# Entry normalisation of a one-core encoder trunk: ScalarE measures four of nine tiles, VectorE centres and gains in one pass, ScalarE scales after it, GpSimd shifts last, and most mask constants are built later

## The reference, cut to what matters

```
def layer_norm(x, g, b):
    xf = x.astype(F32)
    mu = jnp.mean(xf, -1, keepdims=True)
    var = jnp.mean(jnp.square(xf - mu), -1, keepdims=True)
    return ((xf - mu) * lax.rsqrt(var + LN_EPS) * g.astype(F32) + b.astype(F32)).astype(x.dtype)

xp = layer_norm(x_prompt, ln_in_g, ln_in_b)      # (1, 1024, 1024)
xs = layer_norm(x_sample, ln_in_g, ln_in_b)      # (1, 64, 1024)
```

## Time and profile before

| what | value |
|---|---|
| median of three runs | 2655.39 us |
| span of the profiled execution | 2650.3 us (of the whole execution only this span is recorded) |
| TensorE busy with matmuls | 2431.2 us, 92% |
| VectorE, ScalarE, GpSimd busy | 1923.1, 1373.6, 1339.5 us |
| the entry: first transposition, end of the entry | 15.60 us, 63.64 us after the span's start |

### The profile page before, as it was taken

The page is one execution under the profiler, slowest core; times in us unless marked ns, Lnnn a source line. Parts: engine busy times, 40 slices in busy tenths (PEclk is TensorE's granted clock), DMA queues, the critical chain, the costliest instruction groups (busy, mean ns, idle before and its releaser), DMA issues. The chain is left out here.

```text
span 2650.3 us, 40161 instructions
## 1 busy us (share of the span) xinstructions
PE 2431.2 (92%) x14824; PEld 2183.7 (82%) x14824; DVE 1923.1 (73%) x3073; ACT 1373.6 (52%) x2032; POOL 1339.5 (51%) x1317
## 2 busy tenths in 40 slices
PE   4999999999999999999986999699999999999990
PEld 4889898898998989989875775499989898888980
DVE  7475765757758567575676687578888888888875
ACT  3443625426245263452633332267777777777772
POOL 6354664646546556455564265334555455554320
PEclk9999999999999999999987999799999999999995
DMA  5201111111110111101113323489999999999994
GB/s 183 61 26 33 54 34 45 34 40 46 42 45 28 39 45 39 57 25 41 45 73 115 102 75 134 119 261 285 311 305 310 302 303 311 307 313 313 352 333 162
DMA packets 207582, 380.77 MB, mean 144 GB/s; under 512 B 22694, under 2 KB 129546, under 8 KB 206874
## 3 DMA queue, kind: packets, MB, share of 16 engines
q1 hardware_dynamic: 180330, 302.31, 33.0%
q0 software_dynamic: 25824, 71.42, 11.8%
q10 hardware_dynamic: 1232, 4.46, 0.4%
HBM read 314.84 MB, written 72.97 MB: 146 GB/s over the span
## 5 line engine op out<-in xcount | busy, mean ns | idle before, releaser
L122 PE MATMUL ps<-xTh,w_mix_low 128*128 128x368 f32 (+1 forms) x1728 | 595.8, 345 | 10.2 <-POOL w_mix_low L116 8.8
L123 PE MATMUL ps<-xTl,w_mix_high 128*128 128x368 f32 (+1 forms) x1728 | 569.6, 330 | 0.0
L124 PE MATMUL ps<-xTh,w_mix_high 128*128 128x368 f32 (+1 forms) x1728 | 567.5, 328 | 0.0
L2087 POOL DMA_INDIRECT ys_d<-yo,tab_early x114 | 214.2, 1879 | 426.9 <-DVE yo L2259 263.9
L122 PEld LDWEIGHTS ps<-xTh,w_mix_low 128*128 128x128 f32 x1728 | 326.0, 189 | 21.9 <-issue 18.6
L123 PEld LDWEIGHTS ps<-xTl,w_mix_high 128*128 128x128 f32 x1728 | 326.2, 189 | 9.1 <-issue 6.2
L124 PEld LDWEIGHTS ps<-xTh,w_mix_high 128*128 128x128 f32 x1728 | 325.6, 188 | 0.0
L2129 PE MATMUL ps<-xghl,wgh 128*128 128x320 f32 (+5 forms) x1024 | 271.4, 347 | 13.5 <-DVE xghl L116 6.9
L2129 PE MATMUL ps<-xghl,wuh 128*128 128x320 f32 (+5 forms) x1024 | 263.4, 344 | 0.0
L2131 PE MATMUL ps<-xghl,wgl 128*128 128x160 f32 (+5 forms) x1024 | 240.0, 234 | 0.0
L2131 PE MATMUL ps<-xghl,wul 128*128 128x160 f32 (+5 forms) x1024 | 238.6, 233 | 0.0
(11 more groups left out here) (378 smaller groups left out, 5968.8 us busy)
## 6 DMA issues: line engine op xcount, KB each, us to landing
wd_early<-in_w_exp_down SPq DMA_DIRECT2D x64, 1024.0 KB, 9.2
wg_early<-in_w_exp_gate SPq DMA_DIRECT2D x124, 512.0 KB, 7.5
wu_early<-in_w_exp_up SPq DMA_DIRECT2D x124, 512.0 KB, 5.8
w_mix_raw<-in_w_in SPq DMA_DIRECT2D x72, 512.0 KB, 3.9
mT_d<-gs_m SPq DMA_DIRECT2D x8, 544.0 KB, 2.7
xr_m<-in_x_prompt SPq DMA_DIRECT2D x8, 512.0 KB, 3.7
xn_d<-xr_m SPq DMA_DIRECT2D x8, 512.0 KB, 2.8
out<-vrow_m SPq DMA_DIRECT2D x8, 512.0 KB, 4.8
```

The costliest lines, as they stand in the source:

```text
L122: pe.matmul(out, ll, rh, start=start, stop=False)
L123: pe.matmul(out, lh, rl, start=False, stop=False)
L124: return pe.matmul(out, lh, rh, start=False, stop=stop)
L2087: pool.indirect_dma_start(out=ys_d[:, :], out_offset=rows_of(e, j, m), in_=yo[:m, b, j, :], in_offset=None, compute_op=ALU.add, bounds_che ...
```

## The change

It does five things.

1. Tiles 1, 3, 5 and 7 are measured by ScalarE: a Copy over the tile with an accumulated sum (`entry_total`), a Copy of one column that makes the mean, a Square with the mean as bias and an accumulated sum (`entry_spread`). The even tiles keep bn_stats on VectorE, two tiles ahead of their use. Epsilon comes in as the bias of the square root.
2. VectorE subtracts the mean and multiplies by `g_in` in one scalar_tensor_tensor (`centre`); then it takes the reciprocal. The multiplication L1157 and the one-column instruction L1149 go.
3. ScalarE multiplies by the reciprocal after that (`entry_scale`), ahead of high(t-2) in its list, where the normalisation stood behind it.
4. GpSimd's shift waits for ScalarE's scaling. The first group of weights is split after shift(0), the second after shift(2), and the mask levels come behind shifts 5 to 8 and after the loop.
5. The statistics have a buffer of their own for each tile (`ste`).

```diff
+            BY_SCALAR = (1, 3, 5, 7)
...
+                def entry_total(t):
+                    m = rows(t)
+                    act.wait_ge(x_in[t % 4], 16 * (t // 4 + 1))
+                    act.activation(entry_dump[:m, :], xr[:m, t % 4, :], ACT.Copy, accum_out=ste[:m, t, 14:15]).then_inc(entry_sum, 1)
+
+                def entry_spread(t):
+                    m, n = rows(t), BY_SCALAR.index(t) + 1
+                    stt = ste[:m, t, :]
+                    act.wait_ge(entry_sum, n)
+                    act.activation(stt[:, 12:13], stt[:, 14:15], ACT.Copy, scale=1.0 / D).then_inc(entry_mean, 1)
+                    act.wait_ge(entry_mean, n)
+                    act.activation(entry_dump[:m, :], xr[:m, t % 4, :], ACT.Square, scale=-1.0, bias=stt[:, 12:13],
+                                   accum_out=stt[:, 13:14]).then_inc(entry_square, 1)
...
+                def entry_scale(t):
+                    m = rows(t)
+                    act.wait_ge(scaled, t + 1)
+                    act.wait_ge(inverse_ready, t + 1)
+                    act.activation(xr[:m, t % 4, :], xr[:m, t % 4, :], ACT.Copy, scale=ste[:m, t, 16:17]).then_inc(normed, 1)
+
+                act.wait_ge(memo, 4)
+                entry_total(1)
+                entry_root(0)
+                entry_spread(1)
                 for t in range(NT):
-                    m = rows(t)
-                    stt = st[:m, t % 2, :]
-                    act.wait_ge(var_ready, t + 1)
-                    act.activation(stt[:, 15:16], stt[:, 14:15], ACT.Sqrt).then_inc(rstd_ready, 1)
+                    if t + 1 < NT:
+                        if t and t + 1 in BY_SCALAR:
+                            entry_total(t + 1)
+                            entry_spread(t + 1)
+                        entry_root(t + 1)
+                    entry_scale(t)
                     if t >= 2:
                         high(t - 2)
-                    act.wait_ge(shift_ready, t + 1)
-                    act.activation(xr[:m, t % 4, :], xr[:m, t % 4, :], ACT.Identity, scale=stt[:, 16:17], bias=stt[:, 17:18]).then_inc(normed, 1)
...
+                def centre(t):
...
+                    dve.scalar_tensor_tensor(out=xr[:m, t % 4, :], in0=xr[:m, t % 4, :], scalar=stt[:, 12:13], in1=g_in[:m, :],
+                                             op0=ALU.subtract, op1=ALU.mult).then_inc(scaled, 1)
+                    dve.wait_ge(rstd_ready, t + 1)
+                    dve.reciprocal(stt[:, 16:17], stt[:, 15:16]).then_inc(inverse_ready, 1)
...
+                statistics(0)
                 for t in range(NT):
-                    statistics(t)
-                    if t >= 1:
-                        gain(t - 1)
-                    scale(t)
+                    centre(t)
+                    if t + 2 in by_vector:
+                        statistics(t + 2)
                     if t >= 2:
                         low(t - 2)
...
-                    pool.wait_ge(scaled, t + 1)
+                    pool.wait_ge(normed, t + 1)
...
                 for t in range(NT):
                     shift(t)
-                    if t == 0:
-                        split_due(0)
-                    if 1 <= t < 8:
-                        level(t - 1)
+                    if t in (0, 2):
+                        split_first()
+                    if t >= 5:
+                        level(t - 5)
+                for i in range(4, NL):
+                    level(i)
```

More of the change, by code:

```diff
@@ L354, in mixer @@
             tri = entry_only.enter_context(nc.sbuf_tensor("tri", [P, 2, P], F32))
+            ste = entry_only.enter_context(nc.sbuf_tensor("ste", [P, NT, 20], F32))
         x, pm = sb("x_m", [P, 2, NL + 1, 256]), sb("pm_m", [P, 2, NL + 1, P])
@@ L362, in mixer @@
                        "osb_copied pa pd diff_done exp_done eb_done qe_exp qe_done x_done p_done masked a_done ke_done ke_copied "
-                       "y_done oT_copied su_done s_done sg_done silu_done g_done squares root_ready u_raw merged wo_in wo_high wo_low last_s par_in xr0 xr1 xr2 xr3 var_ready rstd_ready entry_s shift_ready normed scaled xn_ready turned x_high x_low xs0 xs1 xs2 xs3 "
+                       "y_done oT_copied su_done s_done sg_done silu_done g_done squares root_ready u_raw merged wo_in wo_high wo_low last_s par_in xr0 xr1 xr2 xr3 var_ready rstd_ready entry_s inverse_ready entry_sum entry_mean entry_square scaled normed xn_ready turned x_high x_low xs0 xs1 xs2 xs3 "
                        "memo built lb_in lb_act lb_dve high_ready") as (block, (
@@ L368, in mixer @@
                 y_done, oT_copied, su_done, s_done, sg_done, silu_done, g_done, squares, root_ready, u_raw, merged, wo_in, wo_high, wo_low, last_s,
-                par_in, xr0, xr1, xr2, xr3, var_ready, rstd_ready, entry_s, shift_ready, normed, scaled, xn_ready, turned, x_high, x_low,
+                par_in, xr0, xr1, xr2, xr3, var_ready, rstd_ready, entry_s, inverse_ready, entry_sum, entry_mean, entry_square, scaled, normed, xn_ready, turned, x_high, x_low,
                 xs0, xs1, xs2, xs3, memo, built, lb_in, lb_act, lb_dve, high_ready)):
@@ L386, in mixer @@
             EARLY = 4
+            BY_SCALAR = (1, 3, 5, 7)
+            by_vector = [t for t in range(NT) if t not in BY_SCALAR]
+            entry_dump = oT[:, 0:D]
             def destination(kind, h, i):
@@ new lines, in entry_root @@
+                def entry_root(t):
+                    stt = ste[:rows(t), t, :]
+                    if t in BY_SCALAR:
+                        act.wait_ge(entry_square, BY_SCALAR.index(t) + 1)
+                        act.activation(stt[:, 15:16], stt[:, 13:14], ACT.Sqrt, scale=1.0 / D, bias=stt[:, 18:19]).then_inc(rstd_ready, 1)
+                    else:
+                        act.wait_ge(var_ready, by_vector.index(t) + 1)
+                        act.activation(stt[:, 15:16], stt[:, 13:14], ACT.Sqrt, bias=stt[:, 18:19]).then_inc(rstd_ready, 1)
@@ L1135, in statistics @@
                     m = rows(t)
-                    xt, stt = xr[:m, t % 4, :], st[:m, t % 2, :]
+                    xt, stt = xr[:m, t % 4, :], ste[:m, t, :]
                     dve.wait_ge(x_in[t % 4], 16 * (t // 4 + 1))
-                    if t >= 2:
-                        dve.wait_ge(normed, t - 1)
                     for b in range(2):
                         ch(dve.bn_stats(stt[:, 6 * b:6 * b + 6], xt[:, 512 * b:512 * b + 512]))
[L1142 to L1152, removed]
+                    dve.bn_aggr(stt[:, 12:14], stt[:, 0:12]).then_inc(var_ready, 1)
+                def centre(t):
                     m = rows(t)
+                    stt = ste[:m, t, :]
                     if t == 0:
                         dve.wait_ge(par_in, 32)
-                    dve.wait_ge(normed, t + 1)
-                    dve.tensor_tensor(xr[:m, t % 4, :], xr[:m, t % 4, :], g_in[:m, :], ALU.mult).then_inc(scaled, 1)
+                    if t in BY_SCALAR:
+                        dve.wait_ge(entry_square, BY_SCALAR.index(t) + 1)
+                    else:
+                        dve.wait_ge(var_ready, by_vector.index(t) + 1)
+                    dve.scalar_tensor_tensor(out=xr[:m, t % 4, :], in0=xr[:m, t % 4, :], scalar=stt[:, 12:13], in1=g_in[:m, :],
+                                             op0=ALU.subtract, op1=ALU.mult).then_inc(scaled, 1)
+                    dve.wait_ge(rstd_ready, t + 1)
+                    dve.reciprocal(stt[:, 16:17], stt[:, 15:16]).then_inc(inverse_ready, 1)
                 def low(t):
@@ L1165, in _ @@
                 ch = Chain(dve, entry_s)
+                dve.memset(ste[:, :, 18:19], LN_EPS).then_inc(memo, 1)
                 dve.memset(tri[:, :, :], 1.0).then_inc(memo, 1)
@@ L1177, in _ @@
                         evacuate(t - 7, t - 6)
-                gain(NT - 1)
                 low(NT - 2)
@@ L1210, in _, with split_first @@
                 g = 0
+                def split_first():
+                    nonlocal g
+                    pool.wait_ge(arrived[g], 16)
+                    pool.tensor_copy(w.high[:, g, :, :], w.raw[:, g, :, :]).then_inc(rounded, 1)
+                    pool.wait_ge(rounded, g + 1)
+                    split_low(pool, w.low[:, g, :, :], w.raw[:, g, :, :], w.high[:, g, :, :]).then_inc(split, 1)
+                    g += 1
                 def split_due(done):
                     nonlocal g
-                    while g < NG and (g < 2 or S.last[g - 2] <= done):
+                    while g < NG and S.last[g - 2] <= done:
                         pool.wait_ge(arrived[g % 2], 16 * (g // 2 + 1))
-                        if g >= 2:
-                            pool.wait_ge(mm_done, S.last[g - 2])
+                        pool.wait_ge(mm_done, S.last[g - 2])
                         if g < base:
@@ L1327, in level @@
                     keep(v, -hw, [[0, P // (2 * hw)], [1, 2 * hw]], 0)
-                pool.wait_ge(memo, 3)
+                pool.wait_ge(memo, 4)
                 keep(tri[:, 0, :], 0, [[-1, P]], 1)
```

## The result

Over six runs each, the changed kernel took 2662.24 us (median, 2653.56 to 2671.57) and the kernel before 2654.35 us (2652.16 to 2662.25). The ratio is 1.0031, 95% interval 1.0018 to 1.0045: some 8 us slower (5 to 12). The forecast was 2657 with a range of 2649 to 2663, and +2.0 us at the end of the entry. One execution is 1.7 us longer than its span (2671.57 against 2669.8), not 5.1: the median and the span of before belong to different executions.

The account below looks back on a forecast made before the run. TensorE, busy for 92% of a 2650.3 us span and fed in fixed order, was taken to bound the kernel, so the entry's +2.0 us goes through to the end: 2655.4 + 2 = 2657.4, said as 2657, range 2649 to 2663.

Parts of the forecast that it names:

- Case A: Entry as worked forward as a chain: +2.0 us, from -2 to +5, range 2653 to 2661; chance 0.62.
- rival C: Odd tiles send ScalarE through two table loads, and TensorE's idle costs its clock: +6.7 to +7.7, worst 10.2; chance 0.10.
- What bounds the entry: TensorE, busy for 92% of the span, is fed by a fixed-order list; moving its unbroken work's start moves the end equally.
- Tile 4 meets the ring: VectorE's statistics(4) waits 3.3 us for x(4), loaded after store(0); 4 us won at shift(2) are down to 1.
- tiles 6 and 8: Statistics wait for load(6) and load(8) ahead of low halves: fill(0) 37.5 against 37.99, fill(2) 54.2 against 52.2.
- The sum, +2.0 at fill(4): End of the entry: fill(4) at 65.2 against 63.2 in the same working, with an idle 3.5 us before fill(2).
- The first table load: ScalarE at the entry's start: lies before 11.8, beside the wait for the parameters, so not on the path.
- The clock: TensorE behind its idle before fill(2): possible cost, named within the main case's range; 1.0 us after an earlier 3.54 gap.
- A rule against it: ScalarE: by the skill's table sets, Square outside the square root's set means two loads a tile; last stage's trace contradicts.
- Rival B: Entry's feed isn't held: loads land before asked for, VectorE and GpSimd don't exclude each other; -6.3 us; chance 0.13.
- Rival D: Behind the entry: its change is swallowed, as TensorE's next waits are set by something that doesn't move; 0; chance 0.15.

Follow-up runs that it names:

- e1: Changed kernel with nine slots instead of four, tiles 4 to 8 in buffers the entry doesn't use, all loads ahead of the stores; ratio 0.9987 to the kernel before.
- e6: Kernel before with a slot for each of the nine tiles and all loads ahead of the stores; ratio 0.9994 to the kernel before.
- e3: Changed kernel with ScalarE's square-root table loaded ahead of its first wait; ratio 1.0020 to the kernel before.
- e2: Changed kernel with 24 matmuls, result not read, between the transposition of tile 6 and fill(2); ratio 1.0025 to the kernel before.
- e5: Changed kernel, four slots, with all nine tiles measured by VectorE and none by ScalarE; ratio 1.0027 to the kernel before.
- e7: Changed kernel with 12 matmuls, result not read, between the transposition of tile 6 and fill(2); ratio 1.0019 to the kernel before.
- e9: Changed kernel, four slots, with statistics of tile t+2 moved behind the low half of tile t-2 in VectorE's list; ratio 1.0020 to the kernel before.
- e10: Changed kernel with nine slots and all nine tiles measured by VectorE; ratio 1.0001 to the kernel before.
- e8: Changed kernel with nine slots, the square-root table loaded first, and the second weight split behind shift(3); ratio 0.9993 to the kernel before.
- e4: Kernel before with only the second weight split behind shift(2) and mask levels behind shifts 5 to 8 and after; ratio 1.0010 to the kernel before.

## Why the prediction was right in its mechanism and small in its size

- **The number** is inside the range partly by luck. Case A, as worked, ends at 2661 and at +5 for fill(4), below the 2662.24 and the +7.6 measured; the range goes on to 2663 only for rival C's table loads between tiles, and none occurred. C's +6.7 to +7.7 meets the +7.6 mostly by coincidence.
- **What bounds the entry**, and that its end goes through to the end of the kernel: right. The eleven kernels of the table show it.
- **Tile 4 meets the ring; tiles 6 and 8**: right. The waits are at the three statistics named (5.1, 2.2 and 4.2 us; the working had 3.3 for the first). e1 takes nearly all of them away and gets 10 us back; e6 shows no gain by slots alone. shift(1) and shift(2) were foretold for 22.5 and 24.9 and ran from 22.38 to 27.04.
- **The sum, +2.0 at fill(4)**, is mis-sized: +7.6. The parts, in the order of the working:
  - The first table load was put "before 11.8, beside the wait for the parameters". This step failed. The load didn't start before ScalarE's wait for tile 1 was over, and there are two. It also turned round who went first, shift(0) or centre(1), and store(0), which was said to stay at 17.23, came at 18.05. Its price at fill(2) is 0.3 us by e3, too little for one trace of each to show.
  - Of turn(3) 35.3 was foretold and 33.67 came, but nothing waited for it: fill(0) starts 4.29 us after it, with low(2).
  - load(6) was taken 2.8 us behind the issue of store(2), with 3.5 to land. It came 5.1 behind, and landed 4.1 later. With store(2) at 27.75 instead of 28.2 that makes 2.4 us, just what fill(0) is late (39.93 against 37.5). The store's length (from its issue to that of the load that waits for it) goes with the load just ahead of it: issued 0.4 us behind load(5), store(2) took 5.0 to 5.3 us in six traces (changed, e2, e3, e5, e7, e9); stores 0.8 to 0.9 behind a load took 4.2 to 4.6, those 1.7 to 2.4 behind 2.8 to 3.4, and the changed kernel's own store(0) and store(1), with none close ahead, 2.6. That the load delays the store is argued from this; nothing was moved to test it. The working took 2.8 us for a store that it had placed right behind a load.
  - fill(0) was taken as 4.8 us long. It took 5.5, behind an idle 4.29, so turn(4), and with it load(8), came another 0.7 late, and fill(2) with them.
  - The clock: an idle 3.5 us ahead of fill(2) was foretold and its price left out of the sum, with the clock's fall named only as a possible part of A's range. e7 gives 2.7 us, where I had estimated 1.0 to 2.0 from the earlier trace rows. 2.4, 0.7 and 2.7 are 5.8 of the 6.0 by which fill(4) missed its 65.2. The working's own baseline was 0.4 early (63.2 against 63.64), so the difference was missed by 5.6.
- **A rule against it.** Two loads a tile didn't occur: from 11.8 to 70.6 ScalarE shows no table load, with Square, Copy and Sqrt mixed, as in the last stage. Of rival C only the clock's part came true.
- **Rival B**: the two engines do exclude each other (3.30 at 15.81), and loads landed after they were asked for, so the low end wasn't open. **Rival D**: its only sign, a next wait that doesn't move, isn't there.
- **The chances**: slower by over 0.3% had 0.09. The ratio of 1.0031 lies on that bound. With the clock's 2.7 in the sum the forecast would have been +4 to +5.

## What to carry to other kernels

When measuring moves ahead in a ring of buffers, count the round trip that frees the slot (store, its landing, the queue behind it, load, its landing) against the time until the new use, and look at what stands behind the new wait in the same list. Price a foretold gap on TensorE with the clock behind it: here 3.2 us of gap cost 2.7 more. And a part that was meant as a gain can be a loss in another order: the later split and masks alone put fill(4) 3.3 us later (the total's interval is 0 to 5 us), where they brought two excluding instructions into step.

## What the runs showed of the hardware

- The granted clock fell to 0.50 in or right behind gaps of 3.11 to 3.65 us ahead of fill(2) (changed kernel, e5, e9, e10), in one of 2.28 (e8), in one of 5.51 ahead of turn(6) (e4), and in e3 right behind one of 2.02, ahead of turn(6). It stayed at 1.00 with 2.01 ahead of fill(2) (e1), with the gap filled (e2, e7), and in the kernel before with an idle 2.50 us ahead of turn(6) at 51.21. Ahead of turn(3), it stayed at 1.00 with 5.77 (e7) and fell with 6.09 (e2), in the same code. So the length of one gap doesn't tell; what does isn't shown.
- The granted clock can read 1.00 while matmuls start 0.31 us apart instead of 0.17, as in the first part of fill(0) (40 to 43 in the changed kernel).
- A VectorE instruction of 128x1 with two SBUF inputs took 0.16 us alone and 2.33 beside a GpSimd addition (e4).
- Where ScalarE's first instruction is a Copy and the first Sqrt comes later, two tables were loaded, and the first of them waited for the Copy's data (8.07). Without the Copy (e5) there was one load, at 8.32, behind the wait of its square root; in the kernel before the one load stood at 3.05, ahead of that wait.
- A store of 512 KB issued 0.4 us behind a load of 512 KB took 5.0 to 5.3 us until the load that waits for it was issued (six traces), and 2.6 with no load close ahead.
